# Routed experts on one core: weights split into two fp32r parts, against weights read as plain f32 in column tiles

## What is computed

```python
def swiglu(h, w_gate, w_up, w_down):
    return (jax.nn.silu(h @ w_gate) * (h @ w_up)) @ w_down

def moe_swiglu(h, router_w, w_gate, w_up, w_down):
    logits = (xf @ router_w).astype(jnp.float32)
    top_val, top_idx = lax.top_k(logits, TOP_K)          # TOP_K = 2 of N_EXPERTS = 8
    gates = jax.nn.softmax(top_val, axis=-1)
    ...
    ys = lax.map(expert_block, (xs, blk_e)).reshape(n_rows, d)
    ys = ys * buf_g[:, None].astype(ys.dtype)
    out = jnp.zeros((n_tok, d), h.dtype).at[buf_tok].add(ys)
```

## Time and profile before

| | us |
|---|---|
| median of 3 runs (1511.88 to 1512.63) | 1512.29 |
| span of the profiled execution | 1509.4 |
| around the span (median less span) | 2.9 |
| first layer, mixer and cross-attention of the second, routing | 0 to 698.4 |
| eight experts | 698.4 to 1492.9 |
| last share, norm, output | 1492.9 to 1509.4 |

### The profile page before, as it was taken

How to read it: one execution, slowest core, us unless ns; L and a number is a source line. 1 busy time by engine, 2 the same in 40 slices (tenths; PEclk the granted TensorE clock), 3 DMA queues, 4 the chain that set the end, 5 groups by cost and what they waited for, 6 DMA issues and landing times.

```text
span 1509.4 us, 21954 instructions
## 1 busy us (share of the span) xinstructions
PE 1448.8 (96%) x8878; PEld 1271.4 (84%) x8878; DVE 1128.9 (75%) x1088; ACT 955.3 (63%) x1116; POOL 177.5 (12%) x133
## 2 busy tenths in 40 slices
PE   7999999999999999998999999999999999999995
PEld 7979988888889889998999777777777999977774
DVE  4766546666665666457776799999999876789996
ACT  5467446344354575355444698998999545479894
POOL 6200000000005000002000204122040300020400
PEclk9999999999999999998999999999999999999998
DMA  9217524555534065426666799999999866679993
GB/s 369 95 46 304 182 87 155 179 193 192 190 132 154 15 248 199 142 96 251 225 233 248 270 388 421 421 421 421 421 421 421 341 224 251 247 281 409 421 421 130
DMA packets 55138, 387.38 MB, mean 257 GB/s; under 512 B 6368, under 2 KB 6624, under 8 KB 9216
## 3 DMA queue, kind: packets, MB, share of 16 engines
q1 hardware_dynamic: 54112, 384.20, 65.0%
q10 hardware_dynamic: 432, 1.08, 0.2%
q0 software_dynamic: 496, 0.74, 0.1%
HBM read 383.90 MB, written 2.10 MB: 256 GB/s over the span
## 4 chain that ended last, share of the span: by engine, by line
PE 64%; DVE 26%; ACT 5%; issue 4%; DMA 0%; SPq 0%; ACTq 0%; DVEq 0%
DVE w_low L1302 15%; PE banks L1807 10%; PE banks L1808 10%; PE banks L1809 10%; PE banks L2144 7%; PE banks L1980 5%; PE banks L2146 5%; DVE low_more L1302 5%; PE banks L1805 4%; PE banks L1806 3%; PE banks L1982 3%; PE banks L2029 1%; ACT w_high L857 1%; DVE after_heads L1585 1%; PE banks L2015 1%
## 5 line engine op out<-in xcount | busy, mean ns | idle before, releaser
L1302 DVE TENSOR_TENSOR w_low<-raw,w_high 128x2048 fp32r<-128x2048 f32 x258 | 587.5, 2293 | 161.4 <-ACT w_high L857 161.2
L857 ACT ACTIVATE w_high<-raw 128x2048 fp32r<-128x2048 f32 x258 | 492.3, 1920 | 160.2 <-PE banks L1982 65.8
L1805 PE MATMUL banks<-w_high,rows 128*128 128x512 f32 (+1 forms) x424 | 161.6, 387 | 3.0 <-ACT after_heads L1126 2.5
L1806 PE MATMUL banks<-w_low,rows 128*128 128x512 f32 (+1 forms) x424 | 156.8, 376 | 0.0
L2144 PE MATMUL banks<-rows,w_high 128*128 128x320 f32 x544 | 142.5, 307 | 0.8 <-ACT rows L857 0.8
L2146 PE MATMUL banks<-rows,w_low 128*128 128x256 f32 x544 | 142.0, 278 | 0.0
L1807 PE MATMUL banks<-rows,w_high 128*128 128x256 f32 x480 | 137.3, 286 | 2.0 <-DVE rows L1303 2.0
L1807 PE MATMUL banks<-w_high,rows 128*128 128x256 f32 x480 | 137.5, 286 | 0.0
L1808 PE MATMUL banks<-rows,w_high 128*128 128x256 f32 x480 | 136.5, 284 | 0.0
L1809 PE MATMUL banks<-rows,w_low 128*128 128x256 f32 x480 | 136.5, 284 | 0.0
L1809 PE MATMUL banks<-w_high,rows 128*128 128x256 f32 x480 | 135.8, 283 | 0.0
(11 more groups left out here) (239 smaller groups left out, 3257.4 us busy)
## 6 DMA issues: line engine op xcount, KB each, us to landing
raw<-in_pieces_dram SPq DMA_DIRECT2D x291, 1024.0 KB, 7.6
raw_more<-in_pieces_dram SPq DMA_DIRECT2D x66, 1024.0 KB, 9.0
phase<-in_mem_dram SPq DMA_DIRECT2D x2, 1024.0 KB, 6.7
early<-in_constants_dram SPq DMA_DIRECT2D x1, 1088.0 KB, 13.9
h_res<-in_x_dram SPq DMA_DIRECT2D x2, 512.0 KB, 4.4
phase<-in_mix_norm_post_dram SPq DMA_DIRECT2D x2, 512.0 KB, 4.4
phase<-in_xa_norm_post_dram SPq DMA_DIRECT2D x2, 512.0 KB, 6.6
kept<-h_res SPq DMA_DIRECT2D x2, 512.0 KB, 3.1
```

Of the source, the lines that this page charges most:

```text
L857: return act.activation(out_, in_, ACT.Copy, scale=scale)
L1302: return dve.tensor_tensor(out_, in_, plain(high), ALU.subtract)
L1805: pe.matmul(dst, stay[0], move[0], start=start, stop=False, skip_group_check=True)
L1806: return pe.matmul(dst, stay[0], move[1], start=False, stop=stop, skip_group_check=True)
```

## The change

The weights of the experts are no longer split. TensorE reads each piece as plain f32 from the slot where it landed, and a slot is free once TensorE has used the piece (`mixed`). The room of the part buffers becomes 13 more slots: `raw_of_parts` 6, `raw_of_mixed` 2, `raw_more` 5, so 19 in all. The first 8 of the added slots may be filled once the last product of the cross-attention has read its parts, the other 5 once routing is done. Layer 1 and the dense channel mixer keep their parts.

Tokens are gathered from `xn` in one plain f32 product (`gather`), and the copies move 128x512 into `token_rows`. In class 1 a matmul has 64 stationary columns (the tokens) and writes 64 of the 128 PSUM partitions: the two halves of the step's columns go to the two halves of the array. In class 3 the first 128 tokens take a plain 128x512 product, and the 32 further ones (`rest_columns`, `rest_outputs`) take 32 stationary columns in one of four quarters. The turning becomes a transpose; the folding matmuls, the copies for them and the sums of wide blocks (L1531) go.

```diff
-MORE = 2
+OF_MIXED = 2
+MORE = 5
+ADDED = 2 * SPLIT + OF_MIXED + MORE
...
                 if c == more_from:
+                    sp.wait_ge(tile_full, after(DEPTH - 1, "xo"))
+                if c == more_from + ADDED - MORE:
                     keep_h()
-                if c >= more_from + MORE:
-                    sp.wait_ge(low_ready, c - len(ring) + 1)
+                if c >= more_from + ADDED:
+                    wait_mixed(sp, c - len(ring))
...
-                for d in columns:
-                    for h, part in enumerate((xn_high, xn_low)):
-                        for t in range(TT):
-                            ins = pe.matmul(banks[:, at(d), h * SEQ:(h + 1) * SEQ], part[:, t, d * P:(d + 1) * P],
-                                            place[:, t, :], start=(t == 0), stop=(t == TT - 1))
-                    ins.then_inc(gathered, 1)
+                for d in (2 * pair, 2 * pair + 1):
+                    for t in range(TT):
+                        ins = pe.matmul(banks[:, bank, d % 2 * SEQ:(d % 2 + 1) * SEQ], xn[:, t, d * P:(d + 1) * P],
+                                        plain(place[:, t, :]), start=(t == 0), stop=(t == TT - 1), skip_group_check=True)
+                ins.then_inc(gathered, 1)
...
+                def columns(half, s):
+                    kind, dst = ("gate", "up")[half], banks[:, 4 + half, :]
+                    per, w = KT // of_step(s), width(s)
                     for i in range(of_step(s)):
                         c = piece(e, kind, s, i)
-                        wait_parts(c)
...
+                        wait_loaded(pe, c)
+                        wt = view(raw_at(c), 0, per, w)
+                        for k in range(per):
+                            first, last = i == 0 and k == 0, i == of_step(s) - 1 and k == per - 1
+                            if groups == 1:
+                                for h in range(2):
+                                    own = slice(h * HALF_BLOCK, (h + 1) * HALF_BLOCK)
+                                    ins = plain_product(dst[own, 0:w // 2], x[:, i * per + k, 0:HALF_BLOCK],
+                                                        wt[:, k, h * (w // 2):(h + 1) * (w // 2)], first, last)
+                            elif groups < GROUPS:
+                                ins = plain_product(dst[:, 0:w], x[:, i * per + k, 0:P], wt[:, k, :], first, last)
...
+                def rest_columns(half, s):
+                    kind, per = ("gate", "up")[half], KT // of_step(s)
+                    for i in range(of_step(s)):
+                        c = piece(e, kind, s, i)
+                        wt = view(raw_at(c), 0, per, width(s))
+                        for k in range(per):
+                            for q in range(blocks_per_step(s)):
+                                ins = plain_product(banks[q * QUARTER:(q + 1) * QUARTER, 6, half * P:(half + 1) * P],
+                                                    x[:, i * per + k, P:P + QUARTER], wt[:, k, q * P:(q + 1) * P],
+                                                    i == 0 and k == 0, i == of_step(s) - 1 and k == per - 1)
                         ins.then_inc(mixed, 1)
...
+                def rest_outputs(s):
+                    for hh in range(2):
+                        for q in range(blocks_per_step(s)):
+                            own = slice(q * QUARTER, (q + 1) * QUARTER)
+                            wt = view(raw_at(piece(e, "down", s, q // 2)), 0, FPS, D)
+                            ins = plain_product(banks[own, 2 + hh, :], turned[:, quarters_at(s), P + own.start:P + own.stop],
+                                                wt[:, q % 2, hh * HALF:(hh + 1) * HALF], s == 0, True)
```

More of the change, by code:

```diff
@@ L1598, in take_turned @@
                     ins.then_inc(hT_ready, 1)
                 for s in range(WIDE_STEPS):
-                    two = of_step(s) == 2
-                    if blocks == 2 and s:
+                    if s and groups < GROUPS:
                         take_turned(s - 1)
-                    if two:
-                        ahead(piece(e, "gate", s, 0))
-                    if blocks == 1 and s:
-                        take_turned(s - 1)
-                    ahead(piece(e, "gate", s, of_step(s) - 1))
@@ L2052, in columns, with wait_first_rows, plain_product @@
-                def columns(kind, half, s):
-                    per = KT // of_step(s)
+                blocks, bank = blocks_of(groups), rows_bank(groups)
+                x = token_rows[:, e % 2, :, :]
+                def wait_first_rows(i):
+                    pe.wait_ge(x_ready, i + 1)
+                    pe.wait_ge(x_by_dve, i + 1)
+                    if i:
+                        pe.nop().then_inc(x_ready, len(FIRST_BY_DVE))
+                def plain_product(dst, stay, move, start, stop):
+                    return pe.matmul(dst, stay, move, start=start, stop=stop, skip_group_check=True)
@@ L2054, in columns @@
+                def columns(half, s):
+                    kind, dst = ("gate", "up")[half], banks[:, 4 + half, :]
+                    per, w = KT // of_step(s), width(s)
                     for i in range(of_step(s)):
                         c = piece(e, kind, s, i)
-                        wait_parts(c)
-                        wt = weights_of(c, per, width(s))
-                        for b in range(blocks):
-                            for k in range(per):
-                                ins = product(banks[:, bank_of(half, s, b, blocks), 0:width(s)], rows_of(b, i * per + k),
-                                              parts(wt, every, k, every), i == 0 and k == 0,
-                                              i == of_step(s) - 1 and k == per - 1, stacked(b))
@@ new lines, in expert @@
+                    last = s == WIDE_STEPS - 1
+                    if groups == 3 and (last or not s):
+                        rest_columns(0, s)
+                        rest_columns(1, s)
+                    next_rows(s)
+                    if last:
+                        outputs(s - 1, range(1) if groups < 3 else None)
+                        wait_rows_taken(s)
+                        turn(s)
+                        if groups == 3:
+                            rest_outputs(s - 1)
+                        else:
+                            outputs(s - 1, range(1, 2))
+                    elif s:
+                        outputs(s - 1)
+                        if groups == 3:
+                            rest_columns(0, s)
+                            rest_columns(1, s)
+                            rest_outputs(s - 1)
```

681 lines of the change are left out of this document (227 added, 454 removed).

## The result

| | before | after |
|---|---|---|
| median, us | 1512.09 | 1476.16 (1475.13 to 1476.96) |
| span of the profiled execution, us | 1509.4 | 1475.1 |
| after / before | | 0.9761, 95% interval 0.9748 to 0.9775 |

The changed kernel is 36 us faster; the forecast was 1532 us, slower. The time lies at the lower edge of the stated range, on the rival "four quarters abreast" (1475 us).

The account below looks back on a forecast made before the run. TensorE was taken to bound class 3, DVE and transfers class 1. Six class 1 experts win 57.4 us, two class 3 lose 74.8; with start and end +20.0 us on 1512.3 gives 1532 us, range 1470 to 1645.

Parts of the forecast that it names:

- four quarters abreast: Class 3, 32 further tokens: records of different tiles need not hold each other, 57.3 us falls to 28.7; 1475 us; chance 0.17.
- What bounds before: Experts before the change: TensorE bounds class 3 (147.4 and 151.2 us), DVE and transfers together class 1 (81.6 us).
- Prices of plain f32: TensorE records in the experts: 0.429 us for 512 moving columns, 0.216 for 256, about 0.109 for 128.
- Halves at half the serial price: Class 1 products: matmuls in different column halves overlap, half the serial price; gate, up and down together 57.0 us.
- Quarters at half the serial price: Class 3, 32 further tokens: at most two tiles abreast, 38.4 us for gate and up, 18.9 us for down.
- The start: Gathering before expert 0: 7 f32 records at 0.43 us, 25 at 0.216, ending at 701.6, 3.1 us more.
- The end: After the last down pass: the two copies before the share run on ACT and DVE side by side, 0.5 us less.
- The transfers: Experts 1 to 4: (132 - 19) x 2.47 = 279 us of transfers, less than TensorE's 296, so TensorE bounds class 1.
- GB/s below 421: Sign that the forecast is right: the GB/s line falls below 421 at the end of experts 1 to 4.
- the serial case: Rival for the tiled products: halves run one after the other, 0.216 and 0.109 us apart; 1989 us; chance 0.15.
- the exposed loads: Rival: a weight load shows per tiled matmul, records 0.13 to 0.14 us apart; 1629 to 1649 us; chance 0.22.
- The transfers' rival: Class 1: slots free too late to run ahead, experts stay at 81.6 us, +51 us, 1583 us; chance 0.04.

Follow-up runs that it names:

- the next gain on TensorE: Changed kernel with gathering of 64 columns in place of 256 for an expert of at most 64 tokens: 1466.94 us, ratio 0.9717.
- seven orders: Changed kernel's alternating halves and quarters (1476.16 us); runs of two matmuls (1478.44, 1476.77), of four (1549.88, 1522.73); two quarters alternating, then the other two (1482.42).

## Why the prediction was wrong, point by point

- **What bounds before** held: the six class 1 experts were at DVE's and the transfers' pace, 81.6 us. To fall below it they needed both, DVE's passes gone and slots to run ahead: with 8 slots and no DVE passes, experts 2 to 4 and 7 stayed at 81.4 to 83.4 us.
- **Prices of plain f32**, 0.429, 0.216 and 0.109 us a record: held. Written to one tile, 0.4325, 0.2169 and 0.1094 were measured.
- **Halves at half the serial price**: held, 0.1057 us against 0.108. The spare feed given as a reason was an estimate from 0.429 against 0.23 us, a factor of 1.87; the runs show the distances, and none tests a feed. Shape changes at 0.17 us and 26 an expert were right in sum: 72.8 us for the 73.1.
- **Quarters at half the serial price**: the step that failed. "the second record of one tile holds back the first of the next, and two are abreast at most" took an order seen within one tile for an order between tiles. The trace of before could not show the difference: no two of its matmul records start less than 0.027 us apart, and those of the earlier trace rows write one half twice. The term was 38.4 + 18.9 = 57.3 us a class 3 expert; in the trace it is 21.3 us for the columns and 11.0 us for the down products, 32.3 us. That is 25.0 us of the 26.9 by which the window is shorter (158.1 for 185.0); the other 1.9 us lie in smaller terms that no run took apart.
- **The start**: the gathering of expert 0's rows, which ended at 698.4 before, began at 693.5, and the first gate product at 702.4, predicted 701.6. The granted clock, 1.00 in every window of the experts, is 0.50 when this gathering begins: in the kernel before until 696.2, with records of 256 columns 0.213 us apart up to then and 0.120 us afterwards, in the changed kernel until 697.2, with eight distances of 0.427 us and then 0.216. So the predicted 7 records at 0.43 us and 25 at 0.216 have the right prices. The gathering began 0.4 us later than before and the clock rose 1.0 us later, an estimated half of it lost: together near the 0.8 us. **The end**: PE idles 1.0 us ahead of the last share, where before it idled 1.39 us, so 0.4 less for the 0.5 predicted.
- **The transfers**: 279 us for experts 1 to 4 where 296.3 were measured. It cost no more than expert 4's 1.4 us, but the sign "GB/s below 421" was wrong, and the next gain on TensorE ran into it.
- **Rivals**: the serial case (0.216 apart) and the exposed loads (0.13 apart) are excluded by 0.1057; at half of the serial distance there is no room left for a load. The transfers' rival did not come with 19 slots and came in part with 14 and 8. The quarters rival had 0.17 and was right in mechanism and place. Its time (158 for its 156 us, 1476 for 1475) is in part luck, since its 28.7 us count four quarters in the last step too, where the trace has 32.3 in all.

With the measured quarter term the same sum gives 1532 - 2 x 25.0 = 1482 us. The 6 us down to 1476 are the 1.9 us in each class 3 expert, some 1 us at the end, and some 2 us less around the span, less 1 us at the start.

The choice within the bounds was the fault as much as the step: of half and a quarter of the serial price, a factor of two apart, I took the half on an order that no row had tested between tiles, and this term decided the sign.

## What to carry to other kernels

Small stationaries in plain f32 are worth putting in column tiles: two of 64 columns cost half (0.1057 us a record for 0.2169), four of 32 a quarter (0.0270 for 0.1094), if the program alternates between them. Runs of up to two matmuls per tile cost little or nothing (0.1073 and 0.028 us), runs of four lose three to four tenths of the gain (0.139 us for 0.106, where one tile takes 0.217; 0.061 for 0.027, where one takes 0.109). When a second limit is counted in buffers, count those still in use or filling at the start as taken, and what is moved for the next stage at the end: here 19 slots were 17 pieces ahead, and worth 15. An average over all records of a form can mix stages: 0.0294 us hid 0.0270 and 0.0542, and a law fitted to such averages came out wrong.

## What the hardware showed that I had not expected

- Column tiles start independently: by the starts in the trace, records of different tiles begin 0.007 us apart where they alternate, and a later matmul of one tile starts ahead of an earlier one of another (748.09 and 748.20 above).
- Four quarters reach 4.05 of 4 (0.1094 / 0.0270 us), two halves 2.05 (0.2169 / 0.1057). The excess comes from the count, not from the tiles: within one tile records start 0.109 and 0.216 us apart whether or not the others work, but 128 records over four quarters hold only 31 such distances in each, 3.43 us over 127 distances.
- The starts are those of tiles that each take in four f32 records, two matmuls, one at work and three waiting: seven orders and the last step's runs of eight fit this within 0.001 us a record (0.0902 us for 0.090 in the runs of eight).
- A tile that had stood idle takes 0.024 us more for its first 32x128 record (0.133 for 0.109) and 0.051 us more for its first 64x256 record (0.267 for 0.216).
